# Seven block products in place of eight, in three groups of each feed-forward stage

## The reference, cut to what matters

```python
def swiglu(x, w_in, w_out):
    gu = x @ w_in                  # 256x1024 @ 1024x5632
    g, u = jnp.split(gu, 2, axis=-1)
    return (jax.nn.silu(g) * u) @ w_out   # 256x2816 @ 2816x1024
```

## Time and profile before

| | |
|---|---|
| median of the runs | 1617.18 us |
| span of the profiled execution | 1615.2 us |
| PE busy | 1606.5 us (99%), 7562 instructions |
| DVE busy | 940.6 us (58%) |
| ACT busy | 789.6 us (49%) |
| POOL busy | 161.3 us (10%) |
| DMA | 308.02 MB, mean 191 GB/s; SP's queue q1 56.7% of the 16 engines' span |
| TensorE clock granted | mean 0.999 of full speed |

### The profile page before, as it was taken

The page is one execution under the profiler, slowest core; times in us unless marked ns, Lnnn a source line. Parts: engine busy times, 40 slices in busy tenths (PEclk is TensorE's granted clock), DMA queues, the critical chain, the costliest instruction groups (busy, mean ns, idle before and its releaser), DMA issues.

```text
span 1615.2 us, 20528 instructions
## 1 busy us (share of the span) xinstructions
PE 1606.5 (99%) x7562; PEld 1335.9 (83%) x7562; DVE 940.6 (58%) x948; ACT 789.6 (49%) x941; POOL 161.3 (10%) x235
## 2 busy tenths in 40 slices
PE   9999999999999999999999999999999999999998
PEld 7888888888888888888888888888888888888887
DVE  6454656765545645465676554577754556874545
ACT  6444455554444544345555444466543446653444
POOL 1111112011000001111101000031100002110000
PEclk9999999999999999999999999999999999999999
DMA  9767655456655566756555665651665564366562
GB/s 283 254 202 227 214 194 163 164 184 217 203 186 176 189 218 212 228 201 196 170 165 174 232 209 182 201 181 67 215 219 189 173 202 162 105 216 196 167 201 91
DMA packets 209459, 308.02 MB, mean 191 GB/s; under 512 B 12452, under 2 KB 151096, under 8 KB 209400
## 3 DMA queue, kind: packets, MB, share of 16 engines
q1 hardware_dynamic: 205928, 300.66, 56.7%
q0 software_dynamic: 3168, 6.06, 1.4%
q10 hardware_dynamic: 304, 0.50, 0.1%
HBM read 304.00 MB, written 2.88 MB: 190 GB/s over the span
## 4 chain that ended last, share of the span: by engine, by line
PE 99%; ACT 0%; DVE 0%; issue 0%; POOLq 0%; POOL 0%; DVEq 0%; ACTq 0%
PE pg L1924 21%; PE pg L1926 21%; PE pg L1925 21%; PE acc L1924 10%; PE acc L1926 10%; PE acc L1925 10%; PE pg L2043 2%; PE pg L1937 1%; PE acc L2149 0%; PE acc L2131 0%; PE acc L2320 0%; PE acc L2278 0%; PE pg L2320 0%; PE acc L2289 0%; PE acc L2137 0%; PE acc L2116 0%
## 5 line engine op out<-in xcount | busy, mean ns | idle before, releaser
L1336 DVE TENSOR_TENSOR wlo<-raw,whi 128x2048 fp32r<-128x2048 f32 (+1 forms) x267 | 611.6, 2291 | 452.5 <-ACT whi L919 452.2
L919 ACT ACTIVATE whi<-raw 128x2048 fp32r<-128x2048 f32 (+1 forms) x267 | 509.5, 1909 | 318.7 <-PE acc L1926 153.3
L1924 PE MATMUL pg<-whi,xTh 128*128 128x512 f32 (+1 forms) x1456 | 575.4, 395 | 0.3 <-DVE wlo L1364 0.3
L1926 PE MATMUL pg<-whi,xTl 128*128 128x512 f32 (+1 forms) x1456 | 566.4, 389 | 0.0
L1925 PE MATMUL pg<-wlo,xTh 128*128 128x512 f32 (+1 forms) x1456 | 565.7, 389 | 0.0
L1924 PEld LDWEIGHTS pg<-whi,xTh 128*128 128x128 f32 x1456 | 273.4, 188 | 57.8 <-issue 1.7
L1926 PEld LDWEIGHTS pg<-whi,xTl 128*128 128x128 f32 x1456 | 273.2, 188 | 56.5
L1925 PEld LDWEIGHTS pg<-wlo,xTh 128*128 128x128 f32 x1456 | 273.6, 188 | 54.6 <-issue 1.0
L1924 PE MATMUL acc<-whi,bTh 128*128 128x512 f32 (+1 forms) x572 | 228.4, 399 | 0.0
L1926 PE MATMUL acc<-whi,bTl 128*128 128x512 f32 (+1 forms) x572 | 222.8, 390 | 0.0
L1925 PE MATMUL acc<-wlo,bTh 128*128 128x512 f32 (+1 forms) x572 | 221.8, 388 | 0.0
(11 more groups left out here) (241 smaller groups left out, 1064.9 us busy)
## 6 DMA issues: line engine op xcount, KB each, us to landing
raw<-in_ffn_w_in SPq DMA_DIRECT2D x172, 512.0 KB, 4.8
raw<-in_ffn_w_out SPq DMA_DIRECT2D x88, 512.0 KB, 4.2
raw<-in_w_gate_up SPq DMA_DIRECT2D x88, 512.0 KB, 4.6
raw<-in_mix_w_in SPq DMA_DIRECT2D x64, 512.0 KB, 4.3
raw<-in_w_down SPq DMA_DIRECT2D x44, 512.0 KB, 4.2
raw<-in_w_in SPq DMA_DIRECT2D x24, 512.0 KB, 4.6
raw<-in_mix_w_o SPq DMA_DIRECT2D x16, 512.0 KB, 4.3
raw<-in_w_o SPq DMA_DIRECT2D x16, 512.0 KB, 4.4
```

What stands on the lines that cost most here:

```text
L919: act_e.activation(whi[:, slot, 0:cols], raw[:, slot, 0:cols], ACT.Copy).then_inc(s.w_hi_ready, 1)
L1336: v.tensor_tensor(wlo[:, slot, 0:cols], raw[:, slot, 0:cols], f32(whi[:, slot, 0:cols]), ALU.subtract)\
L1924: pe.matmul(dst, xh, wh, start=first and i == 0, stop=False)
L1926: mm = pe.matmul(dst, xl, wh, start=False, stop=last and i == len(pairs) - 1)
```

## The change: what it does

Of the 11 steps of a stage, six are taken together as three groups of two (hidden columns 512 to 1023, 1280 to 1791, 2048 to 2559); the other five stay as they are and are called plain. In a group, x is seen as a 2 x 2 matrix of blocks (token tile by half of the contraction) and the weights as a 2 x 2 matrix of blocks of 512 x 512 (half of the contraction by gate or up). Their product needs eight block products in the ordinary way. The change uses the scheme with seven:

- four sums of x blocks, the forms, once in a stage (`joined_operand`, `form`, split into `form_h` and `form_l`);
- four sums of weight blocks in each group: T1 = gate0 + up0, T2 = T1 + up1, T3 = up0 + up1 by DVE (`first_sum`, `second_sum`, `third_sum`), and T4 = T2 + gate1, made by `added_block`: two DMAs on GpSimd's queue with `accum_op=ALU.add` that add the block in HBM onto T2 in SBUF;
- seven products (`summed(i, 0)` to `summed(i, 6)`, 12 matmuls each), each with a unit of its own to split: gate0, T1, gate1, T2, T3, up1, T4. Products 2 and 6 add onto a bank that holds an earlier one;
- one copy of the first product by ACT (`first_product`) and six combinations of 128 x 512 by DVE (`combine_z`, `_u`, `_w`, `_up1`, `_up0`, `_gate1`), then silu and product 512 wide (`pair_silu`, `pair_product`).

A stage now has 42 units in place of 33, of which 27 are loaded into `raw`; up0 and up1 of a group go to buffers of their own. The loops are written out. The core of the new order on PE, and of DVE's for one group:

```diff
+                for i in range(GROUPS):
+                    if i:
+                        combined(i - 1, UP0_AT)
+                    summed(i, 0, b_x, x_block(0, 0))
+                    plain(2 + i, 0, 0)
+                    if i == 0:
+                        turn(b_y, act, 0, 4)
+                    plain(2 + i, 1, 0).then_inc(s.unit_done, 1)
...
+                    summed(i, 1, b_y, x_form(0))
+                    plain(2 + i, 0, 1).then_inc(s.ffn_t0_done, 1)
+                    plain(2 + i, 1, 1).then_inc(s.unit_done, 1)
+                    pe.wait_ge(s.p1_sb, GROUPS * f + i + 1)
+                    summed(i, 2, b_x, x_block(0, 1), onto=True)
+                    if i:
+                        turn_first(i - 1, True)
+                    combined(i, Z_AT)
...
+                    summed(i, 3, b_y, x_form(2))
+                    down(3 * i, lambda: turn_first(i - 1, False) if i else None)
+                    combined(i, W_AT)
+                    summed(i, 4, b_y, x_form(1))
+                    down(3 * i + 1, lambda: turn_plain(i))
+                    pe.wait_ge(s.silu_ready, ACTS * f + 4 + 4 * i + 3)
+                    summed(i, 5, b_x, x_form(3))
+                    if i < GROUPS - 1:
+                        down(3 * i + 2)
+                    combined(i, UP1_AT)
+                    summed(i, 6, b_y, x_block(1, 1), onto=True)
```

```diff
+                joined_operand()
+                form(0)
+                form(1)
+                form(2)
+                form(3)
                 if not start:
-                    refill(0, rnd + 1)
...
+                    loaded_lo(3)
+                form_lo_part(0)
+                product(0, 0)
+                product(0, 1)
+                form_lo_part(1)
+                first_sum(0)
+                for i in range(GROUPS):
...
+                    combine_z(i)
+                    if i == 0:
+                        summed_lo(i, 3)
+                        third_sum(i)
+                        product(2 + i, 0)
+                    else:
+                        third_sum(i)
+                        product(2 + i, 0)
+                        summed_lo(i, 3)
+                    loaded_lo(DOWN_UNITS[3 * i])
...
```

On GpSimd's queue, and on ACT's, where `pair_silu` stands behind the split of T4 in the last group:

```diff
+            def added_block(name, l, rnd, i):
+
+                pool.wait_ge(s.w_lo_ready, unit(0, rnd) + SUM_UNITS[i][3] + 4)
+                for k in range(2):
...
+                    pool.dma_start(t2[:, 2 * k * BANK:2 * (k + 1) * BANK].rearrange("p (k n) -> p k n", k=2), src, accum_op=ALU.add)\
+                        .then_inc(s.w_added, LOADED)
```

```diff
+                    else:
+                        summed_hi(i, 6)
+                        product_hi(3 * i + 2)
+                        pair_silu(i, 0)
```

More of the change, by code:

```diff
@@ L87, with loads_before @@
 CB_COLS = CB_CONV
+def loads_before(rnd):
+    return rnd - (FFN_ROUNDS - FFN_LOADS) * sum(start + FFN_ROUNDS <= rnd for start in FFN_STARTS)
 def first_constants():
@@ L588, in ffn @@
                 else:
[L589 to L599, removed]
+                    plain(0, 0)
+                    plain(0, 1)
+                plain(1, 0)
+                plain(1, 1)
+                for i in range(GROUPS):
+                    if i:
+                        sp.wait_ge(s.w_sum_ready, SUMS * (GROUPS * f + i - 1) + T3_AT)
+                    up_block(i, 0, up_k0)
+                    gate_block(i, 0)
+                    if i:
+                        sp.wait_ge(s.w_lo_ready, unit(0, rnd) + SUM_UNITS[i - 1][5] + 4)
+                    up_block(i, 1, up_k1)
+                    plain(2 + i, 0)
+                    plain(2 + i, 1)
+                    gate_block(i, 1)
+                    for d in range(3 * i, 3 * i + 3):
+                        if d != 2 + 3 * i or i < GROUPS - 1:
+                            down(d)
+                for d in range(8, STEPS):
+                    down(d)
             for l in range(DEPTH):
@@ new lines, in block_done, with silu @@
+                def block_done(m, t):
+                    if t == 0:
+                        act_e.wait_ge(s.ffn_t0_done, BLOCKS * f + m + 1)
+                    else:
+                        act_e.wait_ge(s.unit_done, unit(0, rnd) + PLAIN_UNITS[m][1] + 4)
+                def silu(m, t):
+                    block_done(m, t)
+                    dst = sg if m < 2 else q_act
+                    if m == 2 and t == 0:
+                        act_e.wait_ge(s.form_lo, FORMS * (f + 1))
+                    act_e.activation(dst[:, t, :], pg[min(m, 1)][t][:, 0:FB], ACT.Silu, scale=rstd[:, t:t + 1]).then_inc(s.silu_ready, 1)
@@ L1009, in ffn @@
                 if f > 0:
-                    refill(0, rnd + 1)
-                act_e.wait_ge(s.ffn_t0_done, STEPS * f + 1)
+                    loaded_hi(3)
+                form_hi_part(0)
                 silu(0, 0)
[L1013 to L1031, removed]
@@ L1831, in mixer_b @@
                 conv_in(0)
-                mla_out(0)
+                mla_out(0, 2)
                 sw_out(1)
@@ L2056, in down @@
                             for n2 in range(2):
[L2057 to L2059 removed]
+                                mm = added(t, d % 2, u % SLOTS, n2, k, d == 0 and k == 0, False)
+                        if t == 0 and amid:
+                            amid()
                     mm.then_inc(s.unit_done, 1)
```

507 lines of the change are left out of this document (395 added, 112 removed).

## The result

The changed kernel takes 1592.07 us (median of 4 runs, 1590.86 to 1592.66) against 1617.2: a ratio of 0.9844, 95% interval 0.983 to 0.9858, 1.6% faster. 1585.5 was forecast. The profiled execution took 1590.86 us at a span of 1589.1, 1.8 above the span (2.0 before). The spans of the changed kernel's eight executions lie between 1587.5 and 1590.9, so differences under some 1.5 us between single profiles say little by themselves.

What follows compares the result with a forecast made beforehand. PE bounds the kernel: matmul count times the distance between them. Span 1615.2 - 49.0 (matmuls gone) + 8.2 (start waits) + 9.1 (first `down` waits) = 1583.5, runs 2.0 above: 1585.5 us; range 1570 to 1610.

Steps and rivals of the forecast that it cites:

- 216 matmuls, 49.0 us: On PE, 84 in place of 96 gate and up matmuls per group, 3 groups, 6 stages, at 0.2267 us each.
- the prediction's own sign: A PE step of three longer than 47.6 us without a wait would mean the 0.2267 us distance does not hold.
- Start waits, 8.2 us: PE's first `turn` waits for block 0's activation: 0.9 us in five stages, 3.7 in the first.
- First `down` of group 0, 9.1 us: PE waits for the low part of the `down` unit, behind T3 on DVE: 1.5 us, six times.
- Adding transfer, 11 us, hidden: T4's transfer on GpSimd's queue: double a plain load's 4.8 us plus 1.4 for issues, costing PE nothing.
- The limit of 15.1 us: In group 2, how long T4's adding transfer may take until PE waits at `summed(2,5)`.
- 22.8: In groups 0 and 1, the us T4's adding transfer may take until PE waits.
- The prediction's own sum for 25 us: Slow adding transfer at 25 us: 15.3 us lost a stage, 92 in all, 1677 us; slower kernel had chance 0.08.
- No waits in groups 1 and 2: T3 fits DVE's idle time ahead of the first `down`, 0.7 us in hand; smallest margin elsewhere 0.5 us.
- DVE at 1300 us: DVE's busy time rises from 941 to about 1300 us, about 60 us more per stage, summed by durations.
- the distance of 0.2267: PE's us per matmul, from 12 matmuls in 2.72 us on ACT's timeline, at the upper clock level.
- "No waits", 1568: Rival: start and first `down` waits are swallowed, 1617.2 - 49.0 = 1568 us; chance 0.15, with all up to 1578.

Runs made afterwards that it cites:

- the order experiment: Against the changed kernel, at each stage's start DVE made plain block 0's two products ahead of the forms, ACT its two silu ahead of form 0's high part: 1586.06 us.
- the address runs: Against the kernel with third sum first and start order changed (1576.27 us), forms 2 and 3 moved 160 or 3744 bytes on in the work area: 1573.55 and 1573.34 us.
- the run with the forms swapped: Against the changed kernel, forms 0 and 1 exchanged places with forms 2 and 3 between their two tensors, same instructions and order: 1591.37 us.
- the run that adds twice: Against the changed kernel, each group's adding transfer was issued twice, the second after the first had landed, so the result differs: 1687.91 us.

## Why the forecast was near, and where it fell short

- *216 matmuls, 49.0 us.* Right. A group with its plain step takes 47.84 us in the trace (402.79 to 450.63), 47.6 was forecast; 24 matmuls of form products at 7 ns are 0.17 of the difference. A step longer than 47.6 without a wait was the prediction's own sign that the distance does not hold for all matmuls, and it pointed to the right place.
- *Start waits, 8.2 us.* 0.755 x 5 + 3.67 = 7.4. Right by mechanism (the 0.43 us from PE's last start to ACT is in no row shown, but in the trace of before: 45.10 to 45.53); the order experiment removed the five of 0.755 and only split the sixth.
- *First `down` of group 0, 9.1 us.* 1.50 x 6 = 9.0, and 9.3 of span came back when its cause was undone.
- *Adding transfer, 11 us, hidden.* 10.4 to 12.9 us from the first issue to the last landing. No row had shown such a transfer; doubling the plain load was a guess, and it held (6.1 against 3.0 us of engines per MB), while the two issues take 2.44 where I took 1.4. The limit of 15.1 us was exact in the group looked at, and over all six groups 2 to within 1 us; 22.8 was up to 2.6 us too wide in group 1. (The prediction's own sum for 25 us, 2.4 + 3.0 + 9.9, does not fit a limit of 22.8 in both groups either, which gives 2.2 twice.) The price of passing them was too low: I had no term for the clock.
- *No waits in groups 1 and 2.* Right; the margins from 0.5 us on held, since DVE's pieces of 128x2048 stayed at 2.28 to 2.31 us in the mean (single ones took up to 3.16).
- *DVE at 1300 us.* 1274: I added durations, and in a row they overlap by 0.08 each, some 4 us a stage.

What fell short is the sum: it had terms for matmuls that go and for waits, and took the distance of 0.2267 as the same for all that stay. Span forecast 1583.5, measured 1589.1, 5.6 more. In order:

- waits 0.9 less than forecast;
- the form products +3.0 (432 x 7 ns; shown by the address runs, where 2.7 to 3.5 came back);
- the lower clock level behind the first stage's pause +1.4 (slow transposes, then three or four matmuls at 0.42). It is gone in the start-order run, which has no such long pause, and also in the run with the forms swapped, which has it;
- a longer first distance behind each `down` wait (391.78 to 392.09 is 0.31), +0.5;
- matmuls close behind a wait, a transpose or a form product, +0.7. In both kernels some of the next ten start 229 to 236 ns apart, and 1791 matmuls of the changed kernel lie that close where before had 1505.

That leaves 0.9 unplaced. The distance of all other matmuls did not change: more than ten matmuls behind such a place it is 226.7 ns in the mean in both kernels (4552 of them before, 3591 after). The mean over the products on xTh and xTl grew from 227.25 to 227.52 only because fewer of them lie so far from one; it is the same without the adding transfers.

"No waits", 1568, was a fair rival for the wrong reason: nothing was swallowed, but most of the two waits could be ordered away (3.6 us of the first stage stay), and with the forms' address the kernel comes to 1573.3 to 1573.6, 2.7% under before.

## What to carry to other kernels

Lay out the queues and look for idle time of the late engine just ahead of the step that PE waits for: 2.2 us of work that stood behind such a gap and not in it cost 9 us in six stages. Where the engine is full, moving work only splits the wait: 3.7 us became three of 3.6 together, and what it gave, under 1 us, was the lower clock level behind the long pause. A sum of a loaded block and one in SBUF can go to a free queue if it has twice a load's time, with room for the spread (two in a row took 20.5 to 28.4 us here); on the busy engine, at the one place tried, the same sum cost 18 us.

## What the chip showed that was not expected

- An operand's address changed TensorE's distance between matmuls by 7 ns of 227: (addresses are the allocator's) 234.0 at byte 172512 of a partition, 232.9 at 172544, 227.4 to 227.8 at 172672, 176256 and 90240. In an engine bound by matmul count this is worth a look at every new tensor.
- In the run that adds twice, each of eleven pauses of 3.6 us or more cost TensorE another 1.2 to 2.2 us at the lower clock level, and none of 2.6 or less brought it. One pause of 3.6 us in the run with the forms swapped did not bring it either. So waits are not priced by their length alone.
- GpSimd's two issues of a pair of adding transfers took 2.44 us, 1.2 us per 512 KB, against 0.53 for the plain 64 KB ones before.
